# Seven buffers instead of four for the context's first 126 gathered rows

## The reference

```
h = rmsnorm(x) * (1 + scale1) + shift1
u = short_conv(h @ w_in)                      # r, k, v and the Hyena inputs
ya = rwkv scan, forward and backward          # 8 heads, the context's final state is an output
yb = Hyena long convolution over cos/sin products
x = x + gate1 * (concat(ya, yb) @ w_out)
h2 = rmsnorm(x) * (1 + scale2) + shift2
# PEER: 8 heads, 16 of 16384 single-neuron experts for each head and token
act = gelu(h2 . peer_u[idx]) * gate           # 128 experts for a token
x = x + gate2 * sum(act * peer_v[idx])
y = rmsnorm(x)
```

## Time and profile before

| | |
|---|---|
| median of 3 runs | 2637.39 us |
| the runs | 2637.39, 2640.93, 2623.78 us |
| span of the profiled execution | 2634.3 us, 43615 instructions |
| mean granted TensorE clock | 0.934 of full |
| first gather starts | 691.1 us |
| DVE handles u rows (L1904) | 716.8 to 1113.4 us, 128 rows |
| DVE handles v rows (L1908) | 1121.2 to 1427.6 us |
| L1974 closes units 3 to 9 at | 713.5, 770.5, 823.7, 877.6, 932.0, 986.3, 1038.1 us |
| `ftab` from issue to landing | 9.0 us, 2 MB |
| `hv` back from memory | 10.2 us, 3 MB; `itab` 16.0 us, 2 MB |
| gathers from issue to landing (L2240) | min 4.9, median 6.4, max 16.1 us |

### The profile page before, as it was taken

One profiled execution on the slowest core, in us unless ns is written; L12 is line 12 of the kernel. 1 busy time (PEld: TensorE's weight loads), 2 busy tenths in 40 slices (PEclk: granted clock), 3 DMA queues, 4 the chain that ended last, 5 costly groups with the idle time before them and its releaser, 6 DMA issues.

```text
span 2634.3 us, 43615 instructions
## 1 busy us (share of the span) xinstructions
PE 2362.0 (90%) x18034; PEld 1656.0 (63%) x18034; DVE 1772.4 (67%) x3464; ACT 497.0 (19%) x1002; POOL 938.1 (36%) x774
## 2 busy tenths in 40 slices
PE   5998977888878887999889889999999999999997
PEld 2544545766767776334468777776776777775664
DVE  0111254335677785587689886789899888876767
ACT  2111123324334432100122211000000100000101
POOL 0000000000144443154441003766665666774653
PEclk8998987988989997999899869999999999999998
DMA  9233041130165665286896006999999999999997
GB/s 307 96 112 144 0 143 42 31 131 2 60 220 192 213 209 190 114 312 242 293 366 227 17 33 244 371 394 384 404 408 360 408 409 409 405 395 412 409 409 310
DMA packets 199455, 647.01 MB, mean 246 GB/s; under 512 B 25222, under 2 KB 27142, under 8 KB 198298
## 3 DMA queue, kind: packets, MB, share of 16 engines
q0 software_dynamic: 110592, 402.70, 40.5%
q1 hardware_dynamic: 88666, 241.52, 24.5%
HBM read 635.50 MB, written 8.65 MB: 245 GB/s over the span
## 4 chain that ended last, share of the span: by engine, by line
PE 54%; DVE 16%; DMA 15%; issue 7%; POOL 4%; ACT 4%; SPq 1%; DVEq 0%; POOLq 0%; ACTq 0%
DMA arena<-in_peer_v,arena 9%; PE ps L1078 8%; PE ps L1089 8%; PE ps L599 7%; PE ps L1100 5%; DMA arena<-in_peer_u,arena 5%; PE ps L1054 4%; POOL arena L2252 3%; PE ps L1004 2%; PE ps L1019 2%; DVE arena L2078 2%; PE ps L601 2%; PE ps L850 2%; DVE arena L1904 1%; POOL arena L2240 1%
## 5 line engine op out<-in xcount | busy, mean ns | idle before, releaser
L1089 PE MATMUL ps<-arena 128*128 128x512 f32 x1024 | 466.2, 598 | 20.5 <-DVE arena L2117 20.5
L1078 PE MATMUL ps<-arena 128*128 128x256 f32 x2048 | 478.4, 388 | 0.0
L2252 POOL DMA_INDIRECT arena<-in_peer_u,arena x256 | 341.1, 1333 | 341.2 <-DVE arena L1871 186.7
L1078 PEld LDWEIGHTS ps<-arena 128*128 128x128 f32 x2048 | 391.2, 194 | 68.6 <-issue 19.7
L2252 POOL DMA_INDIRECT arena<-in_peer_v,arena x256 | 299.9, 1171 | 202.5 <-DVE arena L2078 142.3
L2078 DVE SCALAR_TENSOR_TENSOR arena<-arena 128x1024 f32<-128x1024 f32 x252 | 315.6, 1282 | 81.3 <-DMA arena<-in_peer_v,arena 80.4
L2240 POOL DMA_INDIRECT arena<-in_peer_u,arena x128 | 152.9, 1195 | 576.8 <-DVE arena L1871 318.4
L1089 PEld LDWEIGHTS ps<-arena 128*128 128x128 f32 x1024 | 194.6, 192 | 219.7 <-issue 212.6
L2073 DVE SCALAR_TENSOR_TENSOR arena<-arena 128x1024 bf16<-128x1024 f32 x256 | 303.8, 1221 | 41.1 <-DMA arena<-in_peer_u,arena 40.1
L1100 PEld LDWEIGHTS ps<-arena 128*128 128x128 bf16 x3072 | 205.9, 156 | 69.6 <-issue 47.0
L1100 PE MATMUL ps<-arena 128*128 128x32 bf16 x3072 | 208.6, 243 | 23.3 <-DVE arena L2110 22.5
(11 more groups left out here) (361 smaller groups left out, 3340.7 us busy)
## 6 DMA issues: line engine op xcount, KB each, us to landing
arena<-in_uT SPq DMA_DIRECT2D x128, 512.0 KB, 6.8
arena<-in_peer_v SPq DMA_DIRECT2D x128, 512.0 KB, 6.8
arena<-in_w_ada SPq DMA_DIRECT2D x12, 2048.0 KB, 13.9
arena<-in_peer_wq SPq DMA_DIRECT2D x12, 2048.0 KB, 10.5
arena<-in_w_in SPq DMA_DIRECT2D x6, 2048.0 KB, 8.0
arena<-in_w_out SPq DMA_DIRECT2D x4, 2048.0 KB, 9.1
arena<-in_peer_u,arena POOLq DMA_INDIRECT x384, 11.1
arena<-in_peer_v,arena POOLq DMA_INDIRECT x384, 11.1
```

Of the source, the lines that this page charges most:

```text
L1078: m = pe.matmul(ps[:, 4 + i % 2, 0:ND], us[i % UB][:, k, :], hTd[:, k, :], start=(k == 0), stop=(k == KD - 1))
L1089: m = pe.matmul(ps[:, 2 * r + c, :], sgel[:, i % SBUFS, P * r:P * r + P], vs[i % VB][:, 512 * c:512 * c + 512], start=(i == 0), stop=(i == ...
L2252: pool.indirect_dma_start(gring[:, n % RING, :], None, a[("peer_u", "peer_v")[e]][0], bass.IndirectOffsetOnAxis(ap=ids[:, t, m:m + 1], axi ...
```

## The change

Gathers 0 to 125 go round seven slots (`CR + EXTRA`). The three added ones lie in the on-chip memory of the scan's latent start state (`sn`), of the context's scan state (`st2[0]`), and at `w_end`, the first kilofloats of the scan inputs of the context tile. `gring_u` is the list of the seven for n < 126, `gring_c` the list of eight from there on, whose last four are reordered so that slot 6 is the same memory in both. Slots 4 to 6 share the semaphores of the later wide ring, so their uses are counted through.

For the memory to be dead POOL waits, before its first gather, for the `new_state` stores (`out_state`), for `sn_ok` and for the context's `gm_ok`. Gather 126 and all after it wait for `gm_ok` = 5; before, that wait stood at gather 130. SP waits for 125 handled rows before it loads `g2` and `ftab`, which are written into the region in which `sn` and `st2[0]` lie.

```diff
@@ -73,7 +73,7 @@
 GROUPS = ND // GRP
 NPART = NKEY // QI
 ROWS = (GT - 1) * 2 * SLOTS
-CR = 4
+CR, EXTRA = 4, 3
 WIDE_FROM, WIDE_TO = 126, 238
 
 
@@ -81,7 +81,7 @@
 
     slots, last, uses, out = 2 * CR, {}, {}, []
     for n in range(2 * SLOTS):
-        k = n % CR if n < WIDE_FROM else (n - WIDE_FROM) % slots if n < WIDE_TO else (n - WIDE_TO) % CR
+        k = n % (CR + EXTRA) if n < WIDE_FROM else (n - WIDE_FROM) % slots if n < WIDE_TO else (n - WIDE_TO) % CR
         out.append((k, last.get(k), uses.get(k, 0) + 1))
         last[k], uses[k] = n, uses.get(k, 0) + 1
     return out, [uses[k] for k in range(CR, slots)]
@@ -254,7 +254,8 @@
         sif_c = rt(2 * EXPH, TOPK)
         tsum_c = rt(2 * EXPH)
         cand_c = rt(EXPH, TOPK * TOPK)
-        gring_c = [at(x.offset + i * D, D) for i in range(CR)] + [at(w_end + i * D, D) for i in range(CR)]
+        gring_c = [at(x.offset + i * D, D) for i in range(CR)] + [at(w_end + i * D, D) for i in (1, 2, 0, 3)]
+        gring_u = gring_c[0:CR] + [at(sn.offset, D), at(st2[0].offset, D), at(w_end, D)]
         acc_c = [at(x.offset + 4 * D, D), at(hT_at + 4 * D, D)]
         junk_c = [v.bitcast(mybir.dt.bfloat16)[:, 0:D] for v in acc_c]
         hTl = at(hT_at, KD, LL)
@@ -461,6 +462,7 @@
             sp.wait_ge(S("ld_hy"), 3 * 16)
 
             sp.wait_ge(S("unit_ok"), len(UNITS))
+            sp.wait_ge(S("c_used"), WIDE_FROM - 1)
             sp.dma_start(g2, a["rwkv_g2"][0]).then_inc(S("ld_g2"), 16)
             sp.dma_start(ftab, a["ftab"]).then_inc(S("ld_tab"), 16)
 
@@ -1899,7 +1901,7 @@
                     dve.wait_ge(c_here[k], 16 * use)
                     if c >= 2:
                         dve.wait_ge(S("c_used"), c - 1)
-                    slot, dst = gring_c[k], acc_c[c % 2]
+                    slot, dst = (gring_u if c < WIDE_FROM else gring_c)[k], acc_c[c % 2]
                     if e == 0:
                         m = V.scalar_tensor_tensor(junk_c[c % 2], slot, 1.0, h2_c, ALU.mult, ALU.mult, accum_out=dots_c[:, m:m + 1])
                     elif m < 2:
@@ -2230,14 +2232,17 @@
             pool.memset(sn, 0.0).then_inc(S("sn_zero"), 1)
 
             pool.wait_ge(S("eid_ok"), 1)
+            pool.wait_ge(S("out_state"), 16 * 16)
+            pool.wait_ge(S("sn_ok"), 1)
+            pool.wait_ge(S("gm_ok"), 1)
             for n in range(2 * SLOTS):
                 e, m = divmod(n, SLOTS)
                 k, prev, use = C_SLOTS[n]
                 if prev is not None:
                     pool.wait_ge(S("c_used"), prev + 1)
-                elif k >= CR:
+                if n == WIDE_FROM:
                     pool.wait_ge(S("gm_ok"), NT)
-                pool.indirect_dma_start(gring_c[k], None, a[("peer_u", "peer_v")[e]][0],
+                pool.indirect_dma_start((gring_u if n < WIDE_FROM else gring_c)[k], None, a[("peer_u", "peer_v")[e]][0],
                                         bass.IndirectOffsetOnAxis(ap=ids_c[:, m:m + 1], axis=0)).then_inc(c_here[k], 16)
 
             pool.wait_ge(S("h2T_ok"), KD)
```

## The result

The changed kernel takes 2590.33 us (median of 4 runs, 2589.28 to 2594.09) where the kernel before took 2635.4 us beside it: a ratio of 0.9835, interval 0.981 to 0.986. 2584.4 was forecast, 5.9 us less than measured. The profiled execution's span went from 2634.3 to 2588.5 us. Most lines after the ring's definition move by 2 (L1904 is now L1906, L866 is L868), POOL's gather by 5 (L2240 is L2245).

The account below looks back on a forecast made before the run. DVE and POOL were taken to wait on each other through a four-slot ring too short for bursts, stalling PE. Terms 21.7 + 7.0 + 2.5 + 18.7 + 3.1 = 53.0 us off 2637.4 gave 2584.4 us, range 2567 to 2608.

Parts of the forecast that it names:

- First bursts, 21.7 us: Units 4 to 8: seven ready rows outlast a gather's 7.1 us, removing DVE's first-burst waits; 21.7 us, bounds 11 and 22.7.
- PE's clock in the units, 7.0 us: Units 4 to 8: with PE's idle before L689 shrunk, matmuls run at the upper clock; 1.4 us each, 7.0 us.
- The rival by which the clock doesn't come back: Stalls go, but PE's remaining short idles still let the clock fall: 35.4 us won, 2602 us; chance 0.14.
- Second bursts, 2.5 us: Units 4 to 8, second burst: part of the 1.17 us margin to PE's L866 is won, 0.5 us each, 2.5 us.
- Unit 9's L897 8.1 us earlier: Unit 9: PE's L897 starts at 1019.1, when L888 ends, without its 8.10 us idle; 8.1 us, lower bound 4 less.
- the other ten come at the pace of the loop: Unit 9: after seven ready rows, ten arrive every 1.2 us, allowing 1.3 to 1.6, so they end at 1011 to 1014.
- The starved-POOL rival: Back-to-back DVE rows shut POOL out of a seven-row burst, so refills come late: slower, 2646 us; chance 0.05.
- The clock in unit 9 and its tail, 3.4 + 5.2 + 2.0 us: Full clock behind the removed idle: L897 and L899 win 3.4 us, first filters 5.2, gate rows 2.0.
- the prediction's sign: Unit 9's tail: the first filters, 12.97 us before, should take under 8 us.
- The border, 3.1 us: Border of u and v: gathers 126 to 131 go before hv's and itab's loads; PE regains 2.55 plus some 0.5 us.
- The new waits, nothing: POOL's three new waits and SP's wait for 125 rows cost nothing, being met before they matter.
- ftab wasn't late: After unit 9: ftab loads in some 9 us against about 11 us of filters and gate rows, so L961 isn't held up.

Follow-up runs that it names:

- the added matmuls: Changed kernel plus 22 unread 128-column matmuls in PE's idle places of unit 9: ratio 0.9925, run again 0.9941, with the `joined` instructions also moved 0.9946.
- chip C: Chip where the kernel before took 2652.74 us: changed kernel unedited 0.9934, with unit 9 matmuls 0.9941, with first 126 gathers of half the bytes 0.9904.
- A and B: Two chips. First: four slots 1.0002, five 1.0027, six 1.0055, seven with gather 127 held back 0.9945. Second: matmuls added and/or `joined` moved, 0.9925 to 0.9963.
- the first comparison: Changed kernel, unedited, beside the kernel before (2635.4 us): 2590.33 us, ratio 0.9835.
- chip D: Chip where the kernel before took 2636.56 us: changed kernel with gather n waiting until gather n-4 lands, 2592.7 us, ratio 0.9837.

## Why the prediction was right, and where it was not

- **First bursts, 21.7 us.** Right: 22.4 us. In unit 7 from the unit's start to L1638/L1640 it went from 15.1 to 10.6 us, 4.5 us; unit 4 gained more, 5.8 us.
- **PE's clock in the units, 7.0 us.** Right in the mechanism and a little small: between L1640 and L1666 unit 7 went from 13.98 to 12.61 us, 1.37 us, but over the five units it is 8.8 us, 2.9 of them in unit 4. The rival by which the clock doesn't come back is out for this place. What the forecast didn't have is the clock's fall at the start of units 6 to 8; it makes DVE wait 0.3 us for PE before L1640 and costs little.
- **Second bursts, 2.5 us.** Nearly right. From L1666 to L1952 unit 7 went from 13.54 to 12.40 us, 1.14 us: the whole margin of 1.17 us up to PE's L866, not half of it. It gave 0.5 us back behind that. Over the five units 3.2 us are left. With these, units 4 to 8 gained 34.4 us for 31.2.
- **Unit 9's L897 8.1 us earlier.** 5.8 us (40.95 to 35.12 us from the unit's start). The step that failed is "the other ten come at the pace of the loop": the first of them stood 7.41 us in POOL's issue. The starved-POOL rival was right about what happens, in one first burst of six, and not about when: its condition, rows back to back, is met in units 4 to 8 as well, where the issues got through. The two `joined` instructions before unit 9's rows decide it, and neither forecast nor rival had them, though the kernel before already shows 3.98 us there.
- **The clock in unit 9 and its tail, 3.4 + 5.2 + 2.0 us.** This is the step that failed. Between L899's first product and the unit's end 2.2 us were won, and the filters and gate rows took 1.1 us more instead of 7.2 less. The step assumed that with the idle of 8.10 us gone the clock would stay up. There were three idles of about 2 us instead, and it fell behind the second; the first filters took 14.02 us, where the prediction's sign was under 8. The size of the filters' and gate rows' part, 7.2 us, was right: with the clock at 1.00 that stretch was 6.8 to 7.9 us shorter with the added matmuls, and 6.8 us shorter on chip C without them.
- **The border, 3.1 us.** 3.5 us measured; holding the gathers back gave 2.3 us away.
- **The new waits, nothing.** Shown by the ring of four with them: 1.0002.
- ftab wasn't late: it was issued at 995.1 us and landed 7.9 us later, 10.7 us before PE's first L963.

The shortfall in unit 9 and its tail is 11.8 us (6.9 for 18.7), the surplus elsewhere 3.2 + 0.4, 1.7 us came before the end of unit 3, which is luck, and 0.7 were lost later: 7.2 us too much forecast against the span. The median lies 1.8 us above the span here, 3.1 before, which makes it 5.9.

What the prediction didn't have: that the result depends on where or when the kernel runs. Unedited it was worth 0.66% on chip C, and with small edits 0.5 to 0.75% on A and B. There PE and ACT come late while gathers run densely, and more so the deeper the ring. That the forecast came so near is in this sense luck: on chip C the medians differ by 15.7 us, where 53.0 were forecast. What differs stays open, and so does whether it is the count of gathers, their bytes or both. Untested is also whether other work on the same chip plays a part: the two comparisons without "issue" are those in which one kernel alone was compared with the kernel before, while three or four were on each of A to C.

## What to carry to other kernels

Count what a stall costs twice: its own length, and the time at the lower clock behind it; and promise the second only after looking for idles of about 2 us behind the one that goes. A ring's depth should cover the longest burst, not the mean. Look at the issuer's row in each burst: one issue longer than the others, here 3.98 us before the change, names the place where a deeper ring won't help, and what stands before that burst may be the cause. Repeat the unedited kernel on another chip before explaining an experiment by its edit.

## What the runs showed of the hardware

- A gather's issue on POOL took 0.94 us alone and 1.7 to 2.0 us beside DVE's rows. In unit 9, behind the two `joined` instructions, it took 3.98, 5.12, 6.27 and 7.41 us with four to seven slots; with them moved it took 1.68 us. Bursts in units 4 to 8 let it through.
- On chip C PE stood idle in the middle of matmuls that wait for nothing: 54 matmuls in 15 us against 343 in the same stretch of the program, at DMA shares of 0.92 to 0.99 in both. The time called "issue" in units 4 to 8 grew with the ring on chip A, 4.1, 11.3 and 16.1 us, and was absent in the first comparison and on chip D. The cause isn't shown.
- Sixteen small matmuls in an idle of PE, which compute nothing that is used, kept the clock at the upper level for the matmuls behind it; over five units that stretch was 7.7 us shorter.
